# Gate rows as three bf16 parts, a transposed first level, and paired score products in a two-block transformer kernel

## What is computed

```python
g = jnp.cumsum(to_chunks(g), axis=-1)
decay = jnp.exp(jnp.where(causal, g[..., :, None] - g[..., None, :], -jnp.inf))
lower = jnp.where(strict, jnp.einsum('bhncd,bhnsd->bhncs', k_beta, k) * decay, 0.0)
sol = solve_triangular(lower + I, [v * beta, k_beta * jnp.exp(g)])
attn_intra = jnp.where(causal, jnp.einsum('bhncd,bhnsd->bhncs', q, k) * decay, 0.0)
```

## Time and profile before

| what | value |
|---|---|
| median of 3 runs | 2795.44 us (2795.07 to 2797.79) |
| the profiled execution | 2793.53 us |
| its span | 2791.8 us |
| PE busy | 2681.0 us, 96% |
| DVE, POOL, ACT busy | 45%, 41%, 24% |
| mean granted clock of TensorE | 0.977 |

### The profile page before, as it was taken

The page is one execution under the profiler, slowest core; times in us unless marked ns, Lnnn a source line. Parts: engine busy times, 40 slices in busy tenths (PEclk is TensorE's granted clock), DMA queues, the critical chain, the costliest instruction groups (busy, mean ns, idle before and its releaser), DMA issues. The chain is left out here.

```text
span 2791.8 us, 36816 instructions
## 1 busy us (share of the span) xinstructions
PE 2681.0 (96%) x13971; PEld 2123.4 (76%) x13971; DVE 1257.7 (45%) x1789; ACT 663.3 (24%) x1265; POOL 1142.7 (41%) x912
## 2 busy tenths in 40 slices
PE   7999789999999999999999888899999999999998
PEld 6786447888888888887887666763788888888877
DVE  3133443323344333463351255657224556666658
ACT  3201552200000000142232233355122111111123
POOL 5341135244444444552554311222324555555553
PEclk9999999999999999999999978999999999999999
DMA  3111103111111111121111000000311111111112
GB/s 130 44 49 38 46 1 121 31 46 53 45 49 49 48 49 49 57 93 52 46 49 49 1 2 2 17 1 1 121 31 46 53 45 49 49 49 49 49 57 76
DMA packets 91025, 131.74 MB, mean 47 GB/s; under 512 B 9269, under 2 KB 57632, under 8 KB 90920
## 3 DMA queue, kind: packets, MB, share of 16 engines
q1 hardware_dynamic: 88288, 121.76, 14.5%
q10 hardware_dynamic: 2632, 8.51, 0.8%
HBM read 121.82 MB, written 8.42 MB: 47 GB/s over the span
## 5 line engine op out<-in xcount | busy, mean ns | idle before, releaser
L115 POOL TENSOR_TENSOR w_hi<-w_raw,zero 128x512 fp32r<-128x512 f32 x320 | 379.2, 1185 | 1002.5 <-PE bank L1098 450.5
L1096 PE MATMUL bank<-xt_hi,w_hi 128*128 128x512 f32 x1232 | 479.4, 389 | 0.8 <-DVE x_sb L1329 0.8
L1097 PE MATMUL bank<-xt_lo,w_hi 128*128 128x512 f32 x1232 | 479.3, 389 | 0.0
L1098 PE MATMUL bank<-xt_hi,w_lo 128*128 128x512 f32 x1232 | 479.3, 389 | 0.0
L117 POOL TENSOR_TENSOR w_lo<-w_raw,w_hi 128x512 fp32r<-128x512 f32 x320 | 463.7, 1449 | 25.1
L1433 DVE TENSOR_TENSOR x_sb<-bank,x_sb 128x512 f32<-128x512 f32 x320 | 221.2, 691 | 203.6 <-PE bank L1132 203.2
L1096 PEld LDWEIGHTS bank<-xt_hi,w_hi 128*128 128x128 f32 x1232 | 231.2, 188 | 49.2 <-DVE x_sb L1329 1.2
L1098 PEld LDWEIGHTS bank<-xt_hi,w_lo 128*128 128x128 f32 x1232 | 231.2, 188 | 48.0
L1097 PEld LDWEIGHTS bank<-xt_lo,w_hi 128*128 128x128 f32 x1232 | 231.2, 188 | 48.0
L1391 DVE COPY hidden_raw<-bank 128x512 f32<-128x512 f32 x44 | 30.4, 692 | 326.0 <-PE bank L1098 325.9
L178 PE MATMUL bank<-xt_hi,w_hi 128*128 128x512 f32 x448 | 175.8, 392 | 0.0
(11 more groups left out here) (525 smaller groups left out, 4870.3 us busy)
## 6 DMA issues: line engine op xcount, KB each, us to landing
w_raw<-in_w_gate_up_dram SPq DMA_DIRECT2D x88, 256.0 KB, 3.1
w_raw<-in_w_ffn_up_dram SPq DMA_DIRECT2D x88, 256.0 KB, 3.1
w_raw<-in_w_mix_in_dram SPq DMA_DIRECT2D x56, 256.0 KB, 2.7
w_raw<-in_w_down_dram SPq DMA_DIRECT2D x44, 256.0 KB, 2.6
w_raw<-in_w_ffn_down_dram SPq DMA_DIRECT2D x44, 256.0 KB, 2.6
w_raw<-in_w_in_dram SPq DMA_DIRECT2D x40, 256.0 KB, 2.6
x_sb<-in_x_dram SPq DMA_DIRECT2D x4, 1024.0 KB, 8.3
gate_rows<-gate_sums SPq DMA_DIRECT2D x8, 512.0 KB, 6.6
```

The costliest lines, as they stand in the source:

```text
L115: pool.tensor_tensor(m.w_hi[:, u, :], m.w_raw[:, u, :], zeros, ALU.add).then_inc(m.hi_done, 1)
L1096: pe.matmul(m.psum[b][:, :], u_hi[:, col], m.xt_hi[:, k, tok], start=k == 0, stop=False)
L1097: pe.matmul(m.psum[b][:, :], u_hi[:, col], m.xt_lo[:, k, tok], start=False, stop=False)
L1098: mm = pe.matmul(m.psum[b][:, :], u_lo[:, col], m.xt_hi[:, k, tok], start=False, stop=k == KD - 1)
```

## The change

- `sel` is bf16 with 96 rows. The gate rows are split on DVE into three bf16 parts that add up to the float32 value, on partitions 0, 32 and 64 of `gate_thirds`. Rows 4 to 7 of `gc` now hold the log of beta, by a running sum that restarts at every token there. The selector's columns 4 to 7 take decay and log beta together, so `GBb` comes as a sum. All this stands on DVE behind the scan of `gc`.
- `gb` also adds a causal mask in PSUM, by a bf16 product of the identity with `later_b`; POOL makes that mask anew at the start of the projection.
- The per-token column is ACT's bias, so `elt` and `ea` are eight ACT instructions (in halves `elt0`, `elt`, `ea0`, `ea`) and no DVE step for `elt`; `ea` on DVE is one addition of the mask over 128x1024.
- `el`, the second half of `rk`, and the DVE step `X` are gone. `xi` makes X by transposing XT: 16 float32 products of 64x64 on PE, between `w` and `u`, and an ACT copy of 128x512.
- The tables put the steps elsewhere; for later heads `LT` moves from the head's end to level 5.
- In the 16 masked steps both heads' score products are issued, and then both mask products.
- `sel` is no longer made on POOL in the first stage.

```diff
-    PE_SLOTS = {(2, 0): [("ssc", 1)], (2, 1): [("g", 1)], (3, 0): [("gb", 1)], (3, 1): [("ssq", 1)],
-                (4, 0): [("ssk", 1)], (4, 1): [("kt", 1)], (5, 0): [("vt", 1)], (6, 0): [("kk", 1)]}
+    PE_SLOTS = {(2, 0): [("ssc", 1)], (2, 1): [("g", 1)], (3, 0): [("gb", 1)], (3, 1): [("ssk", 1)],
+                (4, 0): [("ssq", 1)], (4, 1): [("kt", 1)], (5, 0): [("vt", 1)], (6, 0): [("kk", 1)]}
...
-    DVE_SLOTS = {(1, 0): [("a_t", 0)], (1, 1): [("qe", 0)], (3, 1): [("gsum", 1)], (4, 0): [("rq", 1)],
-                 (4, 1): [("b", 1), ("rk", 1)], (5, 0): [("vb", 1), ("elt", 1)], (5, 1): [("el", 1)], (6, 0): [("ea", 1)]}
+    DVE_SLOTS = {(1, 0): [("a_t", 0)], (1, 1): [("qe", 0)], (3, 0): [("gsum", 1)], (3, 1): [("b", 1)], (4, 0): [("rk", 1)],
+                 (4, 1): [("rq", 1)], (5, 0): [("vb", 1)], (5, 1): [("LT", 1)], (6, 0): [("ea", 1)]}
...
-    PE_FIRST = ["ssk", "ssc", "kk", "ssq", "kt", "vt", "kq"]
+    PE_FIRST = ["ssk", "ssc", "kk", "ssq", "kt", "vt", "xi", "kq"]
...
-    PE_END = [("w0", 0), ("w1", 0), ("u0", 0), ("u1", 0), ("kq", 1)]
-    DVE_END = [("LT", 1), ("X", 1), ("XT", 1)]
+    PE_END = [("w0", 0), ("w1", 0), ("xi", 1), ("u0", 0), ("u1", 0), ("kq", 1)]
+    DVE_END = [("XT", 1)]
...
+                elif n == "xi":
+                    dve_at(pe, h, "XT")
+                    for c in range(NT):
+                        for rows in (UPPER, LOWER):
+                            mm = pe.matmul(m.psum[2][rows, c * B:(c + 1) * B], XT[rows, c, :], eye[rows, :], start=True, stop=True)
...
+                elif n == "xi":
+                    pe_at(act, h, "xi")
+                    act.activation(X[:, :, :], blocks(m.psum[2]), ACT.Copy).then_inc(act_s, 1)
+                    for c in range(4) if n[-1] == "0" else range(4, NT):
+                        ins = act.activation(t[:, c, :], t[:, c, :], ACT.Exp, bias=small[:, 2, c:c + 1])
...
-                dve_at(pe, h, "X")
+                act_at(pe, h, "xi")
...
-                    if b >= 4 * g:
-                        mm = pe.matmul(m.psum[bank][:, c0:c0 + P], m.ident_b[:, :], mneg[:, :], start=False, stop=True,
-                                       skip_group_check=True)
-                    mm.then_inc(z_made, 1)
+                    if b < 4 * g:
+                        mm.then_inc(z_made, 1)
+                if b >= 4 * g:
+                    for u, h, bank, g, b in units(p):
+                        pe.matmul(m.psum[bank][:, c0:c0 + P], m.ident_b[:, :], mneg[:, :], start=False, stop=True,
+                                  skip_group_check=True).then_inc(z_made, 1)
```

More of the change, by code:

```diff
@@ L1706, in wait_bank @@
                     pe.wait_ge(evac, 8 * c)
[L1707 removed]
+                    pe.wait_ge(rows, 4)
+                    for i in range(2):
                         for x in range(2):
[L1709 removed]
+                            mm = pe.matmul(m.psum[4 + 2 * i + x][:, :], m.sel[:, 4 * i, :], thirds[:, x * HALF:(x + 1) * HALF],
                                            start=True, stop=True)
+                            if i:
+                                mm = pe.matmul(m.psum[4 + 2 * i + x][:, :], m.ident_b[:, :],
+                                               m.later_b[:, :].unsqueeze(1).to_broadcast([P, 4, P]),
+                                               start=False, stop=True, skip_group_check=True)
                         mm.then_inc(spread, 1)
@@ L1809, in vector @@
         step(dve.memset(r2[:, :].rearrange("p (c n) -> p c n", n=P)[:, :, 0:1], 0.0))
+        step(dve.tensor_scalar(r2[:, :], r2[:, :], col8[:, 4:5], None, ALU.mult))
+        step(dve.scalar_tensor_tensor(r3[:, :], ab[:, :], col8[:, 5:6], r3[:, :], ALU.mult, ALU.add))
         dve.tensor_tensor_scan(gc[:, :], r2[:, :], r3[:, :], 0.0, ALU.mult, ALU.add).then_inc(rows, 1)
+        dve.wait_ge(rows, 3)
+        step(dve.memset(thirds[:, :], 0.0))
+        step(dve.tensor_copy(r2[:, :], gc[:, :]))
+        for i in range(3):
+            step(dve.tensor_copy(third[:, :], r2[:, :]))
+            step(dve.tensor_copy(thirds[32 * i:32 * i + 8, :], third[:, :]))
+            if i < 2:
+                step(dve.tensor_tensor(r2[:, :], r2[:, :], third[:, :], ALU.subtract))
+        step(dve.tensor_tensor(heads[:, 0:8], m.ident[0:96, 0:8], m.ident[0:96, 32:40], ALU.add))
+        step(dve.tensor_tensor(heads[:, 0:8], heads[:, 0:8], m.ident[0:96, 64:72], ALU.add))
+        step(dve.tensor_tensor(heads[:, 8:12], heads[:, 4:8], heads[:, 0:4], ALU.add))
+        step(dve.tensor_copy(m.sel[:, 0:4, :], heads[:, 0:4].unsqueeze(2).to_broadcast([96, 4, P])))
+        dve.tensor_copy(m.sel[:, 4:8, :], heads[:, 8:12].unsqueeze(2).to_broadcast([96, 4, P])).then_inc(rows, 1)
         dve.wait_ge(turned, 1)
@@ L1877, in delta_stage @@
     Qb, Kb = (at(n, [P, NT, P], 104 + 4 * i) for i, n in enumerate(("Qb", "Kb")))
-    masks = at("masks", [P, 3, P], 112)
+    mask = at("mask", [P, P], 112)
     lev = at("levels", [P, 6, P], 113.5)
@@ L1960, in _ @@
             pool.memset(eps128[:, :], EPS * P).then_inc(made, 1)
-            pool.memset(masks[:, :, :], 0.0).then_inc(made, 1)
+            pool.memset(mask[:, :], 0.0).then_inc(made, 1)
             pool.memset(lev[:, :, :], 0.0).then_inc(made, 1)
@@ L2207, in _ @@
                         if h + ahead < HG:
-                            prepare(h + ahead, n)
+                            if n == "LT":
+                                start(h + ahead, n)
+                            else:
+                                prepare(h + ahead, n)
                     if h == HG - 1 and g and 2 <= j < 6:
@@ L2216, in _ @@
                 if h + 1 < HG:
-                    for n in ("LT", "X", "XT"):
-                        start(h + 1, n)
+                    start(h + 1, "XT")
         @block.tensor
```

142 lines of the change are left out of this document (68 added, 74 removed).

## The result

The changed kernel took **2764.98 us** in the median of 4 runs (2763.41 to 2766.94) against 2795.26 for the kernel before in the same comparison. The ratio is 0.9887, with a 95% interval of 0.9875 to 0.9900: faster by 1.1%. Forecast were 2763.5 us and a range of 2746 to 2783. The profiled execution took 2766.32 us, its span is 2764.6.

A forecast was written before the change was run, and what follows sets the result against it. PE, busy for 96% of the span, was taken as the bound. Terms -5.1 - 6.8 - 9.0 + 1.5 - 7.9 + 2.4 - 7 = -31.9 took 2795.4 to 2763.5 us, range 2746 to 2783.

The forecast's parts named there:

- Projection: -5.1: Projection chunk 6: bf16 gate products gain 2.6 us by length and 2.5 by clock; bounds -2.6 and -5.5.
- the rival that rested on busy time alone: Projection and levels: clock follows how busy PE has been, so the 2.5 and -9.0 would be 0; chance 0.22.
- Levels 2 to 5: -6.8 and -9.0: Heads 0 to 2: shorter g and gb give -6.8; half the 17.8 us lost to the clock returns, -9.0.
- Boundaries: +1.5: Three head boundaries, 18.8 us on average before: 17.3 to 19.2 at full clock; +1.5 in all, bounds -4.5 and +11.
- I take +0.5 each: Head boundaries: +0.5 us each, after 17.3 to 19.2 at full clock and up to 22.5 with idle stretches.
- Level 1: -7.9: Level 1 of heads 1 to 3: no wait for LT's corner, so 5.5 us each; bounds -4 and -8.
- Start: +2.4: Start of head 0: kq no longer fills PE's wait, about half covered; longer exponentials cost nothing; bounds 0 and +5.
- Attention: -7: Masked attention steps: pairing score products saves 13.3 us of PE, of which 7 is taken; bounds -3 and -13.
- So 9 is near what can be had before DVE is the bound: Attention: of 13.3 us saved on PE, about 9 can be had, as DVE waited 9.2 us for scores.
- The clock stays low: Whole kernel: without the 9.0 and 2.5 us of clock the sum is -20.4, 2775 us; chance 0.22.
- everything returns: Whole kernel: all 17.8 us of clock and 13.3 of attention return, -47, 2748.5 us; chance 0.20.
- the two slower cases: Boundaries become one chain at 1.2 GHz, 2802 us, chance 0.04; or the gains vanish, 2792 us, chance 0.04.

The follow-up runs named there:

- the pair of kernels with 96 and 8 rows: Changed kernel with 16 extra bf16 gate products in chunk 6, over 96 rows or over 8 rows: 2767.26 and 2770.05 us, one run each.
- The float32 kernel: Changed kernel with the gate rows again in float32, selector of 8 rows and no bf16 parts: 2791.55 us (ratio to before 0.998).
- 64 columns: Changed kernel with the eight column sums of k squared made 64 columns wide instead of one: 2766.02 us (ratio to before 0.9885).
- kq first: Changed kernel with kq ahead of xi on PE at head 0's start, and ACT's copy of X ahead of er1: 2755.88 us (ratio to before 0.9854).
- POOL late: Changed kernel with POOL's subtractions and weight splits held until 44 of 48 score blocks are weighed, instead of 28: 2757.0 us (ratio to before 0.9856).

## Why the prediction was right, and where it was not

**Projection: -5.1, measured -5.6.** Right by its own steps. The four products and two masks start 0.22 us apart as taken, and the clock is 1.00 where it was 0.50. The reason given, full-height products among dense ones, is shown by the pair of kernels with 96 and 8 rows. The rule set against it (the Trainium skill, TensorE: Matmul & The Clock Gate, Part 1) speaks of how busy PE has been; the profile's busy share was full in both kernels and only the height differed. So the rival that rested on busy time alone failed there.

**Levels 2 to 5: -6.8 and -9.0, measured -17.3.** Right in sum, and near in the split: the clock's lack fell from 17.8 us to 7.9 (0.18 of 25.8, 0.07 of 23.45 and of 23.47), so 9.9 came back for the 9.0 given. The row for head 0 missed: 25.8 us at 0.82, since level 1 there waits 6.22 us and the low stretch begins earlier. Its clock is below the 0.85 that the prediction had named as a sign of being wrong. That the single-column products keep a low stretch alive is not shown: 64 columns changed nothing in head 1 and moved the stretch to the boundary in head 2. The float32 kernel says that the gate rows alone are worth 21.4 here (8.1 of length for the 6.8 forecast, 13.3 of clock for the 9.0), and the rest of the change cost 4.1 in the levels, which no term had. The two misses cancel for the most part, so the near hit is partly luck.

**Boundaries: +1.5, measured +5.0.** The working at full clock (17.3 to 19.2 us) was right. The kernel with float32 gate rows has the same boundaries, and its first one ran at 1.00 and took 17.54 us:

```profile
1648.13:1665.67 17.54, 12.14 (x160) 11.19 (x160) 9.13 (x13) 6.09 (x15) 5.91 (x3) 1.00 0.01 2
```

The failed step is "I take +0.5 each": it gave the clock next to nothing, though the same paragraph had 22.5 us "where the idle stretches lower it". The granted clock was 0.75, 0.69 and 0.91, and two of the three lay outside the 18 to 20 us that were to show it right. With kq first the same boundaries came to 57.1 us, only 0.7 above before, so most of the miss is where the low stretches fell in this one trace. `xi` waited 0.7 to 1.6 us for XT, not 2 to 4, as `w1` behind the second corner was itself late. The mechanism, POOL's exclusive hold, was right: taking it away gave 8.0 us, of which 4.4 are DVE's time. The other 3.6 are clock, and the kernel with kq first got 4.3 of clock here without any edit at the boundaries.

**Level 1: -7.9, measured -8.3**, at 5.39 us each for the 5.5 taken.

**Start: +2.4, measured +1.8**, by luck of two errors. Up to level 1 it was +5.45, past the upper bound of 5: the exponentials, put "beside `kt` and `vt`: nothing", stood on the path, and moving them gave 5.6 us. Against that, level 1 of head 0 became 3.6 us shorter, which no term had.

**Attention: -7, in the traces -4.0, by experiment -11.** The step that failed is "So 9 is near what can be had before DVE is the bound". With POOL late DVE's round ends no wait of PE above 1.05 us after the first step, and the pairing is worth 17.7. What limited it was POOL's splits holding DVE out, 6.1 us of PE's idle time, which the text had read in the earlier trace rows for the delta stage and not looked for here. The other miss is the base: one execution of the kernel before had a low stretch of 10.2 us where the same order can have 24.

**The total** came within 1.5 us of the forecast, partly by luck. Against the sum of -31.9 the traces have -28.4: boundaries +3.5, attention +3, levels -1.5, and about -0.5 in each of the other three, where the start hides errors of +3 and -3.6. The medians are 30.3 apart because the two profiled executions lay on different sides of theirs. "The clock stays low" was wrong at both places, "everything returns" half wrong, and the two slower cases did not come near.

## What to carry to other kernels

Products of few rows can cost more than their own length: here the clock fell behind them, for 6.8 us behind 16 of 8 rows. Where a row has to be spread over partitions, splitting it into bf16 parts on otherwise empty partitions was worth 26.6 us here, some three fifths of it clock. When a change takes slack from an engine, look up which other engine's work makes its instructions wait, everywhere and not only where the change is: POOL's work had been nearly free until DVE had to be on time, and a later start gave 8 us in one place and 12 in the other, part of both by the clock. And where the clock has two levels, price each stage at both, for an edit in one stage moved low stretches in the next ones, where one edit lost two thirds of its gain and another got twice its own size on top.

## What the runs showed of the hardware that was not expected

- With PE busy without a pause, 16 bf16 products of 8 rows brought the granted clock to 0.51 for 6.8 us; 16 of 96 rows left it at 1.00.
- A low stretch can move without a gain. Behind eight column sums of 1 or of 64 columns the levels of head 1 ran at 0.93 (23.45 and 23.47 us); in head 2 those of 64 columns left the levels at 1.00 and the boundary behind them at 0.75 for 0.91, and the two together took 42.5 us either way. Without the sums the levels of heads 1 and 2 ran at 1.00 and all three boundaries took 21.9 us.
- The same code in the same place took different times by the clock alone: a boundary 18.97 to 21.90 us, the score stage 116 to 117 us with a low stretch of 24 us and 110.66 with one of 10.2. The changed score stage took 106.64 us in the kernel with 16 products of 96 rows more and 103.3 in that of 8 rows, though both edits lie some 280 us ahead of it. A median fell by 9.1 us for a step that became 2.7 shorter.
- A 128x128 DVE copy of 0.22 us took 2.37 beside a POOL subtraction of 128x1024 with two inputs, though it reads one input; the earlier trace rows had shown it for a product of two.
